# A hybrid block on one core: the mLSTM head norm as one ones product per head beside the output gate, its last sums one chunk later, and two small pieces of order moved

## What is computed

```python
# _ab_mixer: the mLSTM branch, 4 heads of 256 features
h_a = _mlstm(q, k, v, gi + ifb[:A_HEADS], gf + ifb[A_HEADS:])
h_a = jax.nn.sigmoid(o).reshape(hs) * h_a                                   # output gate
h_a = h_a * lax.rsqrt(jnp.mean(h_a * h_a, axis=-1, keepdims=True) + EPS)    # head norm
h_a = (h_a * mlstm_norm.reshape(A_HEADS, A_HEAD_DIM)).reshape(bsz, t_all, A_WIDTH)
y = jnp.concatenate([h_a, h_b], axis=-1)                                    # h_b: the RG-LRU branch
return y @ w_out

# _mlstm_chunk: the floor below the denominator
h = num / jnp.maximum(jnp.abs(den), jnp.exp(-m_t))[..., None]

# _diff_attend (8 heads): difference of two softmaxes
p = jax.nn.softmax(jnp.where(mask, s, -jnp.inf), axis=-1)
pd = p[:, :, 0] - lam * p[:, :, 1]
return jnp.einsum('bhqk,bhkv->bhqv', pd, vh)
```

## Time and profile before

| what | value |
| --- | --- |
| median of 3 runs | 3831.0 us (3830.91 to 3839.13) |
| profiled execution, its own time | 3843.75 us |
| span from its first to its last instruction | 3842.0 us |
| TensorE busy in the span | 3696.6 us (96%) |
| VectorE, ScalarE, GpSimd busy | 1783.2, 1261.3, 1364.4 us |
| chain that ended last | PE 84%, DVE 10%, ACT 2% |
| mean granted TensorE clock | 0.973 of full |

### The profile page before, as it was taken

The page is one execution under the profiler, slowest core; times in us unless marked ns, Lnnn a source line. Parts: engine busy times, 40 slices in busy tenths (PEclk is TensorE's granted clock), DMA queues, the critical chain, the costliest instruction groups (busy, mean ns, idle before and its releaser), DMA issues.

```text
span 3842.0 us, 55301 instructions
## 1 busy us (share of the span) xinstructions
PE 3696.6 (96%) x20876; PEld 3158.2 (82%) x20876; DVE 1783.2 (46%) x2364; ACT 1261.3 (33%) x2121; POOL 1364.4 (36%) x584
## 2 busy tenths in 40 slices
PE   8999999999998999999999999999999988899998
PEld 8987999999975788888888788888888866578887
DVE  3762244445454544442336542325232599654224
ACT  3642332223145222232223442224222433643222
POOL 3330234443310344534443044444444400043443
PEclk9998999999996999999999999999999999999999
DMA  4220122222210222322232022222222212022222
GB/s 144 77 72 17 66 78 88 93 89 83 83 39 1 74 97 93 108 73 94 93 104 89 23 77 97 95 93 94 94 97 95 94 66 72 1 94 82 97 95 82
DMA packets 86432, 307.51 MB, mean 80 GB/s; under 512 B 9568, under 2 KB 11872, under 8 KB 86112
## 3 DMA queue, kind: packets, MB, share of 16 engines
q1 hardware_dynamic: 85824, 303.75, 23.3%
q10 hardware_dynamic: 416, 1.05, 0.1%
HBM read 302.67 MB, written 2.10 MB: 79 GB/s over the span
## 4 chain that ended last, share of the span: by engine, by line
PE 84%; DVE 10%; ACT 2%; DVEq 2%; issue 1%; POOL 0%; DMA 0%; ACTq 0%; POOLq 0%; SPq 0%
PE psum L378 66%; PE psum L590 6%; DVE y_space L2664 2%; PE psum L628 1%; PE psum L608 1%; DVE arena L2686 1%; PE psum L1406 1%; PE psum L1393 1%; PE psum L1747 1%; DVE arena L1264 1%; DVE w_lo L2669 1%; PE psum L2060 1%; DVE arena L1295 1%; PE psum L1731 0%; PE psum L2024 0%
## 5 line engine op out<-in xcount | busy, mean ns | idle before, releaser
L342 POOL TENSOR_TENSOR w_lo<-w_raw,w_hi 128x1024 fp32r<-128x1024 f32 (+1 forms) x483 | 1204.1, 2494 | 2153.0 <-ACT w_hi L330 2152.9
L330 ACT ACTIVATE w_hi<-w_raw 128x1024 fp32r<-128x1024 f32 (+1 forms) x507 | 533.5, 1052 | 1846.2 <-PE psum L378 1835.3
L378 PE MATMUL psum<-x_hi,w_hi 128*128 128x512 f32 (+1 forms) x2744 | 909.3, 360 | 33.6 <-DVE w_lo L2669 30.7
L378 PE MATMUL psum<-x_lo,w_hi 128*128 128x512 f32 (+1 forms) x2744 | 905.6, 359 | 0.0
L378 PE MATMUL psum<-x_hi,w_lo 128*128 128x512 f32 (+1 forms) x2744 | 901.5, 357 | 0.0
L378 PE MATMUL psum<-y_hi,w_hi 128*128 128x264 f32 (+1 forms) x2272 | 635.1, 329 | 11.8 <-DVE arena L1273 3.4
L378 PE MATMUL psum<-y_lo,w_hi 128*128 128x264 f32 (+1 forms) x2272 | 635.6, 330 | 0.0
L378 PE MATMUL psum<-y_hi,w_lo 128*128 128x264 f32 (+1 forms) x2272 | 632.7, 328 | 0.0
L378 PEld LDWEIGHTS psum<-x_hi,w_hi 128*128 128x128 f32 x2744 | 488.7, 189 | 123.3 <-DVE w_lo L2669 36.9
L378 PEld LDWEIGHTS psum<-x_lo,w_hi 128*128 128x128 f32 x2744 | 486.7, 189 | 78.4 <-issue 1.4
L378 PEld LDWEIGHTS psum<-x_hi,w_lo 128*128 128x128 f32 x2744 | 487.2, 189 | 76.3
(11 more groups left out here) (475 smaller groups left out, 4383.7 us busy)
## 6 DMA issues: line engine op xcount, KB each, us to landing
w_raw<-in_weights SPq DMA_DIRECT2D x566, 512.0 KB, 3.3
resid<-in_xT SPq DMA_DIRECT2D x8, 264.0 KB, 7.7
out_dram<-resid SPq DMA_DIRECT2D x16, 128.0 KB, 1.7
arena<-in_lru_w SPq DMA_DIRECT2D x1, 1024.0 KB, 10.1
rope_sb<-in_rope SPq DMA_DIRECT2D x1, 528.0 KB, 11.6
mats<-in_mats SPq DMA_DIRECT2D x1, 512.0 KB, 10.5
rope_sb<-in_rope ACTq DMA_DIRECT2D x1, 512.0 KB, 5.1
y_space<-in_pool_inv ACTq DMA_DIRECT2D x1, 512.0 KB, 7.0
```

The lines of the kernel that those rows point to most:

```text
L330: nc.scalar.activation(weight_parts(n, i, c)[0][:, 0:w], RAW[:, (n + c) % 4, 0:w], ACT.Copy).then_inc(high_ready, 1)
L342: nc.gpsimd.tensor_tensor(wl[:, 0:w], RAW[:, (n + c) % 4, 0:w], wh[:, 0:w], ALU.subtract).then_inc(low_ready, 1)
L378: last = mm(o[:, a, :], wt[:, k * P:k * P + P], x[:, k, a * (w // banks):(a + 1) * (w // banks)], start=(k == 0 and p == 0), stop=(k == kt ...
```

## The change

1. **Head norm.** ScalarE squares tile f as soon as VectorE has gated it, which is now done tile by tile, one chunk behind the sigmoid. VectorE adds a head's two squares (`pair`). TensorE sums them and spreads them to all partitions in one step: a 128 by 128 matrix of ones is stationary and the 528 columns of squares move (`squares_sum`, in pieces of 512 and 16). ScalarE takes the root of the mean plus EPS out of PSUM for all 128 partitions (`head_root`), and VectorE the reciprocal of 128 by 528 (`head_share`). The two sums of heads 0 and 1 stand after `o` chunks 4 and 6, those of heads 2 and 3 after `out_lru` chunks 0 and 1. Every `out_lru` chunk then has one normed tile beside it (`normed`, `normed_low`). The steps on columns and the spreading by the identity are gone, and so are the three `heads_` functions. The loops over four chunks on ScalarE are written out.
2. **Floor exponent.** The exponential stands before the split beside the last v chunk. The transposes of the last v tile (`turned(7)`) stand behind `scores(0)` on TensorE and behind `decays(0)` on ScalarE.
3. **Attention's output copies.** `head_out(h-1)` stands in unit i = 1 of the next head, behind `maxima` of the unit after it and ahead of that unit's own reciprocal.

```diff
--- before.py
+++ after.py
@@ -166,9 +166,10 @@
...
-        HSQ = [area(i, 1)[:, 0, :] for i in (26, 27, 28, 33)]
+        HSQ = [area(23 + i, 1)[:, 0, :] for i in range(4)]
+        HROOT = [area(19 + i, 1)[:, 0, :] for i in range(4)]
+        EPS_COL = SM[:, 60:61]
         VCOL, SCOL, RCOL = (COL[:, 8 * i:8 * i + 8] for i in range(3))
...
@@ -1364,8 +1272,6 @@
                                                row[:, P * j:P * j + tail(j)], ident[0:A_HEADS, 0:A_HEADS])
             last.then_inc(st["ml_tr"], 1)
             turned(DT - 2)
-            pe.wait_ge(st["ml_col"], 1)
-            turned(DT - 1)
             def spread_rows(n):
@@ -1423,6 +1329,8 @@
             spread_rows(0)
             spread_rows(1)
             scores(0)
+            pe.wait_ge(st["ml_col"], 1)
+            turned(DT - 1)
             pe.wait_ge(st["ml_vc"], DT)
             for n in range(N_UNITS):
                 if n + 2 < N_UNITS:
...
+            def squares_sum(h):
+                pe.wait_ge(hn_pair, h + 1)
+                if h >= 2:
+                    pe.wait_ge(hn_dev, h - 1)
+                bank = 2048 + 1024 * (h % 2)
+                for a, b in pieces(0, T1):
+                    last = mm(GF[:, bank + a:bank + b], ones[:, :], HSQ[2 * h % 4][:, a:b], start=True, stop=True)
+                last.then_inc(hn_sum, 1)
             product(pe, CHUNKS["o"], 1, YH, YL, follow=True)
             back(N_UNITS - 1)
-            for f in range(1, 4):
+            for f in range(1, DT):
                 product(pe, CHUNKS["o"] + f, 1, YH, YL, follow=True)
-            product(pe, CHUNKS["o"] + 4, 4, YH, YL, follow=True)
-            heads_pe(pe, A_HEADS, 2, 0, 0, T1,
-                     lambda k: product(pe, CHUNKS["out_lru"] + 2 * k, 2, XH, XL, follow=k > 0))
+                if f in (4, 6):
+                    squares_sum(f // 2 - 2)
+            pe.wait_ge(h_low, split_end("lru"))
+            for f in range(2):
+                product(pe, CHUNKS["out_lru"] + f, 1, XH, XL, follow=True)
+                squares_sum(2 + f)
+            for f in range(2, 4):
+                product(pe, CHUNKS["out_lru"] + f, 1, XH, XL, follow=True)
+            product(pe, CHUNKS["out_lru"] + 4, 4, XH, XL, follow=True)
             product(pe, CHUNKS["out_mlstm"], 8, YH, YL, parts=SPLIT_AT["mh"][0])
...
@@ -1460,13 +1385,13 @@
...
             for f in range(DT):
+                if f == DT - 1:
+                    act.wait_ge(st["ml_m"], 1)
+                    nc.scalar.activation(EMR, RL, ACT.Exp).then_inc(st["ml_em"], 1)
                 act_idle(act, CHUNKS["v"] + f, 1)
                 if 0 < f < DT - 1:
                     turned(f - 1)
-            act.wait_ge(st["ml_m"], 1)
-            nc.scalar.activation(EMR, RL, ACT.Exp).then_inc(st["ml_em"], 1)
             turned(DT - 2)
-            turned(DT - 1)
...
             act.wait_ge(st["ml_col"], 1)
             decays(0)
+            turned(DT - 1)
             decays(1)
...
+            def gate_square(f):
+                act.wait_ge(st["ml_gate"], f + 1)
+                if f >= 4:
+                    act.wait_ge(hn_sum, (f - 4) // 2 + 1)
+                nc.scalar.activation(HSQ[f % 4], MQ[:, f, :], ACT.Square).then_inc(hn_sq, 1)
+            def head_root(h):
+                act.wait_ge(hn_sum, h + 1)
+                bank = 2048 + 1024 * (h % 2)
+                nc.scalar.activation(HROOT[h], GF[:, bank:bank + T1], ACT.Sqrt, bias=EPS_COL,
+                                     scale=1.0 / A_DIM).then_inc(hn_dev, 1)
+            for f in range(DT):
+                split_high(act, CHUNKS["o"] + 2, 0, f)
+                act.wait_ge(psum_free, CHUNKS["o"] + f + 1 + 4)
+                nc.scalar.activation(MK[:, f, :], MK[:, f, :], ACT.Sigmoid).then_inc(st["ml_og"], 1)
+                if f:
+                    gate_square(f - 1)
+                if f in (5, 7):
+                    head_root(f // 2 - 2)
+            gate_square(DT - 1)
+            for f in range(DT):
+                split_high(act, CHUNKS["out_lru"] + 2, 0, f)
+                act.wait_ge(h_ready, READY_AT["mh"] + f + 1)
+                nc.scalar.activation(YH[:, f, :], SCR[:, 2 + f % 2, :], ACT.Copy).then_inc(h_high, 1)
+                if f < 2:
+                    head_root(2 + f)
             tail_act(act, CHUNKS["out_mlstm"], "mlp0", [H[:, f, :] for f in range(DT)], T1, True)
...
@@ -1607,15 +1553,54 @@
...
-            take_scaled(dve, CHUNKS["o"], 8, MK)
-            dve.drain()
-            dve.wait_ge(st["ml_og"], DT)
+            def gate(f):
+                dve.wait_ge(st["ml_og"], f + 1)
+                dve.drain()
+                tt(MQ[:, f, :], MQ[:, f, :], MK[:, f, :], ALU.mult).then_inc(st["ml_gate"], 1)
+            def pair(h):
+                dve.wait_ge(hn_sq, 2 * h + 2)
+                sq = HSQ[2 * h % 4]
+                tt(sq, sq, HSQ[2 * h % 4 + 1], ALU.add).then_inc(hn_pair, 1)
+            def head_share(h):
+                dve.wait_ge(hn_dev, h + 1)
+                nc.vector.reciprocal(HROOT[h], HROOT[h])
+            n = CHUNKS["o"]
             for f in range(DT):
-                last = tt(MQ[:, f, :], MQ[:, f, :], MK[:, f, :], ALU.mult)
-            last.then_inc(st["ml_gate"], 1)
-            heads_dve(dve, "mh", MQ, A_HEADS, 2, A_DIM, gains("mlstm_norm", 0), 0, 0, YH, YL, T1,
-                      lambda k: take_add(dve, CHUNKS["out_lru"] + 2 * k, 2, H[:, 2 * k:2 * k + 2, :]))
+                dve.wait_ge(tile_done, n + f + 1)
+                tt(toks(MK[:, f, :], n), acc(n, f), toks(RS[:, :], n), ALU.mult).then_inc(psum_free, 1)
+                if f:
+                    gate(f - 1)
+                if f in (3, 5, 7):
+                    pair((f - 3) // 2)
+                if f == 6:
+                    head_share(0)
+            gate(DT - 1)
+            pair(3)
...
+            def normed(f):
+                dve.drain()
+                stt(SCR[:, 2 + f % 2, :], MQ[:, f, :], gains("mlstm_norm", 0)[f], HROOT[f // 2], ALU.mult,
+                    ALU.mult).then_inc(h_ready, 1)
+            def normed_low(f):
+                dve.wait_ge(h_high, SPLIT_AT["mh"][0] + f + 1)
+                tt(YL[:, f, :], SCR[:, 2 + f % 2, :], YH[:, f, :], ALU.subtract).then_inc(h_low, 1)
+            n = CHUNKS["out_lru"]
+            for f in range(DT):
+                dve.wait_ge(tile_done, n + f + 1)
+                tt(toks(H[:, f, :], n), acc(n, f), toks(H[:, f, :], n), ALU.add).then_inc(psum_free, 1)
+                normed(f)
+                normed_low(f)
+                if f in (1, 2):
+                    head_share(1 + f)
+            dve.drain()
             n = CHUNKS["out_mlstm"]
...
@@ -1903,6 +1888,8 @@
                     if n:
                         dve.wait_ge(st["c_e"], n)
                     maxima(n + 1)
+                if i == 1 and h:
+                    head_out(h - 1)
                 w = META + P * (i + 1)
                 dve.wait_ge(st["c_e"], n + 1)
                 nc.vector.reciprocal(RSUM, SUM1[n % 2])
@@ -1911,8 +1898,6 @@
                 dve.drain()
                 stt(E0[n % 2][:, 0:w], E1[n % 2][:, 0:w], SHARE, E0[n % 2][:, 0:w], ALU.mult,
                     ALU.add).then_inc(st["c_pd"], 1)
-                if i == 0 and h:
-                    head_out(h - 1)
             head_out(C_HEADS - 1)
             dve.drain()
```

98 lines of the change are left out of this document (4 added, 94 removed).

## The result

The changed kernel takes 3783.3 us (median of 4 runs, 3781.3 to 3787.0) against 3832.3 us (median of 4, 3830.9 to 3839.1): a ratio of 0.987 with a 95% interval of 0.9853 to 0.9887, so 49 us less. I had forecast 3808 with a range from 3788 to 3819.

What follows compares the result with a forecast made beforehand. TensorE, busy 96% of the span, was taken as the bound. Head norm 16.2, floor exponent 1.0 and attention's copies 5.5 sum to 22.7 us, taken off the 3831.0 us median: 3808 us, range 3788 to 3819.

Steps and rivals of the forecast that it cites:

- Head norm, 16.2 us: Around `o` and `out_lru`: 20.4 us of TensorE time removed, 4.2 added for four ones products, net 16.2 us less.
- gates' pair: The LRU gates' two products with an fp32 stationary matrix, 2.08 us, used to price each ones product at 1.04 us.
- The last low part: Ready 4.5 us after the last `out_lru` chunk, read by `out_mlstm` 5.1 us after; 0.6 us spare, the thinnest cover.
- second rival: VectorE late beside `out_lru`: TensorE stands some 6 to 10 us for `psum_free`, then `h_low`; 3814 to 3818, chance 0.13.
- sums' wait: Rival in the head norm: each ones product finds its pair not ready, up to 3 us, 12 in all; 3820, chance 0.05.
- Floor exponent, 1.0 us: Ahead of the mLSTM units: a 1.8 us TensorE wait goes, 0.8 us for ScalarE's v copies comes; net 1.0 us less.
- a rival that ends slower: Clock falls in mLSTM units, 16.4 us more per head at 0.50; two heads give 3841 us, chance 0.04.
- Attention's copies, 5.5 us: Attention: TensorE's wait for VectorE's combination falls from 1.31 to 0.4 us; five heads at 0.9, two less, 5.5 us.
- my two reduced heads: Two attention heads with waits of 0.59 and 0.74 us, expected to gain only about 0.4 and 0.6 us, not 0.9.
- my first rival: Attention's clock rises as TensorE's longest idle shortens: up to 24 us more, likelier half; 3796, at the extreme 3784, chance 0.15.
- the small products: Eighty small TensorE products in the old head norm, 13.86 us at a granted clock of 0.50.

Runs made afterwards that it cites:

- norm-alone trace: Kernel before with only the head norm's part of the change: 3817.1 us (6 runs), ratio 0.9949; the trace is of its fastest run.

## Why the prediction was off, step by step

*Head norm, 16.2 us: right.* Between the traces 16.6, and the same in every trace with this part (98.5 us against 115.1 or 115.2 without it); alone 16.0 by medians and 19.5 by the middle of the ratio, in which the pause that moved away may have some 2. Each ones product 1.0 us, as taken from the gates' pair; clock 1.00; no wait for `psum_free` or `h_low`. The last low part was thin but held. The second rival and the sums' wait did not occur.

*Floor exponent, 1.0 us: the waits right, the sum wrong.* The 1.8 us went and the 0.8 came, on the instruction named. Measured alone it is 9.6 us; filling the wait and moving nothing gave 8.3. The step that failed is that I priced a wait of TensorE at its length. At this place the runs show that filling or moving the wait gives most of the time back, not that the wait alone decides: in the norm-alone trace the units lost no more clock behind the same 1.8 us (83.5 us against 83.0). I had looked at the clock in the units only for a rival that ends slower, and there argued from 0.91 in one head; the stretch right behind the wait, at 0.67, I had not read.

*Attention's copies, 5.5 us: the waits right, the sum wrong.* Waits 0.41 where I had 0.4, heads 11.26 where I had 11.3. The chain moved along by 0.9 in all seven, 6.3 and not 5.5: my two reduced heads were an artefact of half clock, where VectorE's lateness is shorter beside slower products. The clock's share, 24 us against the profiled execution and about 14 against an ordinary one if that has three falls, was my first rival, with 0.15. My argument against it, that a head with a wait of only 0.59 us was slow, took the effect for a counterexample: the wait was short because that head was already at half clock. The test for it stood in the prediction (heads under 14 us on average) and came out at 11.3.

*The sum.* 16.2 + 1.0 + 5.5 = 22.7 against 49.0. Of the 26.3 missing, 14.4 are attention (19.9 - 5.5) and 8.6 the floor's part (9.6 - 1.0), both by the traces clock in the main; the 3.3 left are within what the runs can tell, with the pause's 2 us perhaps among them. The single step behind it all is that I took the amount off with the clock held fixed everywhere but in the small products. The Trainium skill ("TensorE: Matmul & The Clock Gate", section "A second HAM failure mode: psum-queue depth-cycling") tells of a kernel in which short idles between groups of matmuls make the clock swing between its two levels and cost throughput. The traces of attention agree: with idles of 1.31 us in most heads the clock is 0.71 over six heads, with 0.41 us it is 1.00.

*The median.* The profiled execution lies 12.75 us over the median, and I left that unexplained. If the median run has three falls, the two more explain 10.2 of them: 111.9 against 101.7.

## What to carry to other kernels

When TensorE is the bound, a wait of one to two microseconds on it can cost more than itself: here 0.9 us off a wait saved 0.9 and about 2 more of clock per head, by the medians. Before pricing it, set heads or tiles that do the same work side by side; where they differ by 40% the short one shows what the stage costs at full clock. A cheap test of whether a stage loses to the clock is to fill the wait with work that changes nothing; if the kernel gets faster, it does. If it doesn't, nothing is proved: one fill here held its own stage's clock and gained nothing. Take more than one trace before you put a number to the clock's share, since one execution can be 11 us from its kernel's median. Don't use a slow stretch as evidence about its own waits, and read the stretch behind each wait that the change touches.

## What the runs showed of the hardware that I had not expected

- More TensorE work made the kernel faster: four products twice in each of seven heads, 17.8 us less.
- With the same code in the heads, executions differ in how many of seven run partly at 1.2 GHz. With waits of 1.31 us it was three or five, with 0.41 none in the traces taken; the changed kernel's four runs lie 6 us apart, those of before up to 20 (8 runs).
- One added instruction of VectorE moved a pause of 0.43 us ("issue", nothing waited for) off a place where it had cost 2.3 us by the order in which two engines reached SBUF. Where the pause went is not seen; what makes it was not tested.
- Filling idle time holds the clock mostly but not always: the same six products gave 1.00 over 310 to 320 us in one kernel and 0.76 in another. With no wait of TensorE from 280 to 400 us at all it was 1.00 from 300 to 304 us in one trace and 0.63 in another.
